# Where the softmax weights of two attention stages are scaled: VectorE before, ScalarE after

## The chip, the core and the metric

The kernel runs on one core of a Trainium2 chip. The metric is the device time of one execution in microseconds (us). Its engines are TensorE (PE in the rows; PEld is its weight load), VectorE (DVE), ScalarE (ACT), GpSimd (POOL) and the queue that issues the loads (SP). Each engine works through its own list of instructions in order; semaphores tie the lists together.

## The reference, cut to what matters

The model is two blocks deep, each with two layers, on 256 tokens of width 1024. The change touches only the attention in the mixer of the second block, which occurs twice (layers 0 and 1, the stages `mix0` and `mix1`). There are 8 heads of 64 and a single key block of 256, so the block selection picks nothing and this is left, causal attention:

```python
s_own = jnp.einsum('bhqd,bhtd->bhqt', qc, k_own) * scale
s_own = jnp.where(k_pos[None, :] <= q_pos[:, None], s_own, NEG_INF)
p = jax.nn.softmax(logits, axis=-1).astype(v.dtype)
...
merged = jax.nn.sigmoid(g_attn) * y_attn + jax.nn.sigmoid(g_conv) * y_conv
return merged @ w_out
```

Beside it the mixer computes a causal convolution of 31 taps over 512 channels, its layer norm, and the projections for q, k, v and the gates.

## The kernel before, in words

Activations lie with channels on the 128 partitions and the 256 tokens along the free dimension. The weights stream in as chunks of 128 x 2048 floats through a ring of three. For every chunk SP loads `raw`, ScalarE rounds it to a high part `wh` (`hi`, L1496), VectorE subtracts to get the low part `wl` (`lo`, L1963), and TensorE multiplies with three products, high by high, high by low and low by high (`three`, L881 to L883). A chunk of a projection is 48 matmuls on TensorE.

A mixer has 18 projection chunks (0 to 17). Chunks 10 to 17 are the gates. Around them the attention is written out by hand in pairs of heads, p = 0 to 3:

- TensorE: `gates(11 + 2p)`, `transposes(p)` (L1378), `scores(p + 1)` (L1367), `gates(12 + 2p)`, `output(p)` (L1386, L1388). `transposes(p)` waits for `pn_made`, the scaled weights of each head.
- VectorE: `masked` (L2478) adds the mask and takes the row minimum, then some taps of the convolution (`convolve`, L2440 and L2430), then `normalise`: the inverse of the two row sums of a head (L2485) and two multiplications by it (L2487), then `lo` of the coming chunks and more taps.
- ScalarE: `exps` (L1848) with the row sums, `gates` (L1630, the sigmoid of the finished chunk, then `hi` of the chunk three ahead), `evacuate` (L1855, the transposed weights from PSUM), `upper` (L1859, the head pair's output).

A head's weights are two pieces, 128 x 128 for the first 128 queries and 128 x 256 for the last. They lie in `mpr[:, h % 2]`, the sums in `rs` and the inverses in `ri`.

The convolution is shared. VectorE has all taps of two of the four channel tiles and the last four taps of the other two; GpSimd has the first 27 taps of these (`pool_mix`, L830 the product, L832 the sum). VectorE's first tap on GpSimd's tiles waits for GpSimd's last sum:

```python
if j == POOL_TAPS:
    dve.wait_ge(pool_step.sem, pool_conv[s])
```

By the order of `taps` that is the third of the five taps that stand between `masked(3)` and `normalise(3)`.

After the loop ScalarE waits until gates 17 are done on TensorE, copies three quarters of the attention output (L1871), evacuates the last pair (L1855), and TensorE can do `output(3)`. TensorE then goes on with the sums for the convolution's norm (L1402) and the next weight chunks, which it waits for in turn.

Of the kernel before, what the change touches and what calls it, by code (L numbers as in the profile page):

```python
# [8 lines left out]
ALU = mybir.AluOpType  # L9
ACT = mybir.ActivationFunctionType  # L10
# [4 lines left out]
P = 128  # L15
# [160 lines left out]
def build(nc, A, out, upto=None):  # L176
# [5 lines left out]
    def signal(name):  # L182
        return Signal(ctx.enter_context(nc.semaphore(name)))
# [37 lines left out]
    rs = sb("rs", [P, 4, 2])  # L221
    ri = sb("ri", [P, 4, 2])
# [172 lines left out]
    score_made = signal("score_made")  # L395
    ns_made = signal("ns_made")
    p_made = signal("p_made")
    pn_made = signal("pn_made")
    pt_made = signal("pt_made")
    pt_out = signal("pt_out")  # L400
# [27 lines left out]
    for kind, s in STAGES:  # L428
        x_of[s] = xstage
        if kind == "rms":  # L430
            for g, n in ((sq_made, KT), (stat_made, 1), (root_made, 1), (rstd_made, 1)):
                g.plan(s, n)
            if s != "rms0":
                six_folded.plan(s, 1)
            if s != "final":
                if s not in DEFERRED:
                    xn_made.plan(s, KT)
                xh_made.plan(s, KT)
                xl_made.plan(s, KT)
            else:  # L440
                x_ready.plan(s, KT)
                xstage = s
        if kind == "even":
            proj_out.plan(s, 12)
            xh_made.plan(s, 1 + 4)
            xl_made.plan(s, 1 + 4)
            x_ready.plan(s, 4)
            xstage = s
            heads_of[s] = 8
        if kind == "odd":  # L450
            proj_out.plan(s, 7)
            raw_made.plan(s, KT)
            xh_made.plan(s, 8)
            xl_made.plan(s, 8)
            x_ready.plan(s, 4)
            xstage = s
            heads_of[s] = 16
        if kind == "mod":
            for g in (xn_made, xh_made, xl_made):
                g.plan(s, KT)  # L460
        if kind == "mix":
            heads_of[s] = 8
            proj_out.plan(s, 18)
            glu_made.plan(s, 1)
            conv_made.plan(s, CONV_K * 2 + (CONV_K - POOL_TAPS) * 2)
            for g, n in ((rope_pe, 4), (rope_dve, 4), (ao_made, 4), (cln_pe, 2), (cln_act, 2 + CT), (cln_dve, 1 + CT),
                         (xh_made, 2 + 2 + 4), (xl_made, 2 + 2 + 4), (merged, 4), (y_out, 4), (x_ready, 4)):
                g.plan(s, n)
            xstage = s
        if kind == "ln":  # L470
            for g, n in ((four_folded, 1), (six_folded, 1), (early_sum, 1), (early_mean, 1), (late_sum, 1), (late_moved, 1), (stat_made, 1), (dsq_made, 1), (var_made, 1), (root_made, 1),
                         (inv_made, 1), (spread, 1), (cen_made, 4), (sq_made, 4), (rstd_made, int(s != STAGES[-1][1])), (ln_made, KT),
                         (x_ready, KT)):
                g.plan(s, n)
            xstage = s
        if kind == "sq":
            y_out.plan(s, KT)
        if s in heads_of:
            for g in (score_made, ns_made, p_made, pn_made, pt_made, pt_out, pv_made):
                g.plan(s, heads_of[s])  # L480
        if kind in ("ffn", "sq"):
            steps = FF_STEPS if kind == "ffn" else FF2_STEPS
            right_out.plan(s, steps * (2 if kind == "ffn" else 1))
            if kind == "ffn":
                for g in (b_made, act_made, gate_scaled, silu_scaled):
                    g.plan(s, steps)
            for g in (a_made, h_made, hh_made, hl_made):
                g.plan(s, steps)
            tile_done.plan(s, 4)
            left_added.plan(s, KT)  # L490
            x_ready.plan(s, KT)
            xstage = s
# [994 lines left out]
    def _(act):  # L1487
# [343 lines left out]
        def act_mix(s):  # L1831
            l, c0 = int(s[3:]), base[s]
            if s == "mix0":
                act.wait_ge(ada_summed.sem, ada_summed.at("ffn3"))
            for step in MIX:
                if isinstance(step, int):
                    act_chunk(s, step, c0 + step, ACT.Sigmoid if step in (2, 3) else ACT.Copy, pm)
                    if step == 1:
                        act_ln_bias(x_of[s])

            def gates(n):
                act_chunk(s, n, c0 + n, ACT.Sigmoid, pm)

            def exps(p):
                for h in (2 * p, 2 * p + 1):
                    act.wait_ge(ns_made.sem, ns_made.at(s, h + 1))
                    for b, at in enumerate((slice(0, P), slice(P, 384))):
                        last = act.activation(mpr[:, h % 2, at], mns[:, h % 2, at], ACT.Exp, bias=nm[:, h % 2, b:b + 1], scale=-1.0,  # L1848
                                              accum_out=rs[:, h % 2, b:b + 1])
                    last.then_inc(p_made.sem, 1)  # L1850

            def evacuate(p):
                for h in (2 * p, 2 * p + 1):
                    act.wait_ge(pt_made.sem, pt_made.at(s, h + 1))
                    act.activation(mpt[:, h % 2, :], bank[6 + h % 2][:, 0:384], ACT.Copy).then_inc(pt_out.sem, 1)  # L1855

            def upper(p):
                act.wait_ge(pv_made.sem, pv_made.at(s, 2 * p + 2))
                act.activation(ao[:, p, :], bank[0][:, 0:T], ACT.Copy).then_inc(ao_made.sem, 1)  # L1859

            gates(10)
            exps(0)
            for p in range(3):
                gates(11 + 2 * p)
                evacuate(p)
                exps(p + 1)
                gates(12 + 2 * p)
                upper(p)
            act.wait_ge(chunk_used.sem, c0 + 18)
            act.wait_ge(ao_made.sem, ao_made.at(s, 3))  # L1870
            act.activation(xh[:, 0:3, :], ao[:, 0:3, :], ACT.Copy).then_inc(xh_made.sem, 1)  # L1871
            evacuate(3)
            upper(3)
            act.wait_ge(ao_made.sem, ao_made.at(s))
            act.activation(xh[:, 3, :], ao[:, 3, :], ACT.Copy).then_inc(xh_made.sem, 1)
            gates(17)
            fetch(ACT.Sqrt)
            act.wait_ge(cln_dve.sem, cln_dve.at(s, 1))
            act.activation(flat(ctmp), flat(cacc), ACT.Square).then_inc(cln_act.sem, 1)
            act.wait_ge(cln_pe.sem, cln_pe.at(s, 2))  # L1880
            act.activation(root[:, :], bank[7][:, 0:T], ACT.Sqrt, scale=1.0 / CW, bias=epsc[:, 1:2]).then_inc(cln_act.sem, 1)
            fetch(ACT.Silu)
            hi(c0 + 18 + RING)
            for ct in range(CT):
                act.wait_ge(cln_dve.sem, cln_dve.at(s, 2 + ct))
                act.activation(ctmp[:, ct, :], cacc[:, ct, :], ACT.Silu, bias=vec(1, V_CLNB + 4 * l + ct)).then_inc(cln_act.sem, 1)
            for q in range(2):
                act.wait_ge(cln_act.sem, cln_act.at(s, 4 + 2 * q))
                act.activation(xh[:, 4 + 2 * q:6 + 2 * q, :], ctmp[:, 2 * q:2 * q + 2, :], ACT.Copy).then_inc(xh_made.sem, 1)
            hi(c0 + 19 + RING)  # L1890
            for i in range(4):
                if i == 2:
                    hi(c0 + 20 + RING)
                act.wait_ge(merged.sem, merged.at(s, i + 1))
                act.activation(xh[:, 2 * i:2 * i + 2, :], xn[:, 2 * i:2 * i + 2, :], ACT.Copy).then_inc(xh_made.sem, 1)
            hi(c0 + 21 + RING)
            act.wait_ge(ada_made.sem, 2 * l + 2)
            act_scaled(s, c0 + 22, l, 2)
# [57 lines left out]
    def _(dve):  # L1956
# [172 lines left out]
        def link(ins):  # L2129

            n_step[0] += 1
            ins.then_inc(dve_step.sem, 1)
            dve.wait_ge(dve_step.sem, n_step[0])
# [280 lines left out]
        def dve_mix(s):  # L2414
# [67 lines left out]
            def normalise(p):  # L2482
                for h in (2 * p, 2 * p + 1):
                    dve.wait_ge(p_made.sem, p_made.at(s, h + 1))
                    link(dve.reciprocal(ri[:, h % 2, :], rs[:, h % 2, :]))  # L2485
                    for b, at in enumerate((slice(0, P), slice(P, 384))):
                        last = dve.tensor_scalar(mpr[:, h % 2, at], mpr[:, h % 2, at], ri[:, h % 2, b:b + 1], None, ALU.mult)  # L2487
                    last.then_inc(pn_made.sem, 1)

            masked(0)  # L2490
            convolve(TAPS_PER_STEP)
# [131 lines left out]
```

## Time and profile before

| | |
|---|---|
| time, median of 3 runs | 1790.83 us (1784.06 to 1793.79) |
| the profiled execution's own time | 1791.12 us |
| its span, first to last instruction | 1789.4 us |
| PE busy | 1742.7 us (97%) |
| DVE busy | 1367.8 us (76%) |
| ACT busy | 936.8 us (52%) |
| POOL busy | 292.7 us (16%) |
| granted TensorE clock, mean | 0.990 of full speed |
| attention pairs of `mix0` / `mix1` | about 1096 to 1154 us / 1474 to 1531 us of the span |

Busy time counts an instruction from start to end; matmuls overlap, so a busy PE is not one at its peak. What counts for the total is what TensorE waits for. The two mixers run the same code, and the times of one repeat in the other, 377.5 us later.

### The profile page before, as it was taken

The numbers are of one execution on the slowest core, as the hardware profiler recorded it, in microseconds if no ns is written. First come the engines' busy times: TensorE is split into PE (matmuls) and PEld (weight loads), VectorE is DVE, ScalarE is ACT, GpSimd is POOL, SyncE is SP. The second block draws the span as 40 slices with busy tenths as digits, with TensorE's granted clock in tenths as the row PEclk, the third lists the DMA queues.
The fourth block names the chain that finished last, engine by engine and source line by source line (L and its number), as shares of the span: only waits on it lengthen the run. The fifth ranks groups of instructions, "written<-read, shape, count | busy, mean of one in ns | idle before, by whom it ended". The sixth has DMA issues, their size and how long they took to land.

```text
span 1789.4 us, 27976 instructions
## 1 busy us (share of the span) xinstructions
PE 1742.7 (97%) x11260; PEld 1565.0 (87%) x11260; DVE 1367.8 (76%) x1830; ACT 936.8 (52%) x1173; POOL 292.7 (16%) x219
## 2 busy tenths in 40 slices
PE   6999999999999999999999999999999999999998
PEld 5888799988888888779888898898888998998887
DVE  5997654798789978686987779878755699778654
ACT  6554464655455544566554444756543536555433
POOL 1000100220210001050000139610000089010000
PEclk9999999999999999999999999999999999999999
DMA  7777433376667766524676643353555344335551
GB/s 270 277 254 268 175 143 118 138 267 259 246 249 290 261 223 247 212 95 174 236 266 247 231 165 141 125 182 129 188 193 193 122 153 157 139 127 200 188 190 48
DMA packets 53232, 348.28 MB, mean 195 GB/s; under 512 B 6769, under 2 KB 10114, under 8 KB 13058
## 3 DMA queue, kind: packets, MB, share of 16 engines
q1 hardware_dynamic: 53122, 346.73, 53.0%
q8 instruction: 80, 1.31, 0.3%
q14 instruction: 30, 0.25, 0.0%
HBM read 345.65 MB, written 1.05 MB: 194 GB/s over the span
## 4 chain that ended last, share of the span: by engine, by line
PE 89%; DVE 7%; ACT 2%; issue 1%; POOL 1%; DMA 0%; SPq 0%; ACTq 0%; DVEq 0%; POOLq 0%
PE bank L926 39%; PE bank L925 21%; PE bank L881 7%; PE bank L882 7%; PE bank L883 7%; DVE wl L1963 2%; ACT wh L1496 1%; DVE bank L2440 1%; PE bank L896 1%; DVE arena L2459 1%; PE bank L1429 1%; PE bank L906 0%; DVE arena L2458 0%; DVE arena L2487 0%; DMA raw<-in_chunks 0%
## 5 line engine op out<-in xcount | busy, mean ns | idle before, releaser
L1963 DVE TENSOR_TENSOR wl<-raw,wh 128x2048 fp32r<-128x2048 f32 (+1 forms) x279 | 640.1, 2296 | 252.7 <-ACT wh L1496 252.0
L926 PE MATMUL bank<-xx,wh 128*128 128x512 f32 x1920 | 674.5, 395 | 0.0
L1496 ACT ACTIVATE wh<-raw 128x2048 fp32r<-128x2048 f32 (+1 forms) x279 | 526.2, 1886 | 204.4 <-PE bank L926 174.0
L925 PE MATMUL bank<-xx,wl 128*128 128x256 f32 x1920 | 541.2, 282 | 14.9 <-DVE wl L1963 14.9
L926 PEld LDWEIGHTS bank<-xx,wh 128*128 128x128 f32 x1920 | 361.1, 188 | 83.4
L926 PE MATMUL bank<-hx,wh 128*128 128x512 f32 x1216 | 422.0, 390 | 0.0
L925 PEld LDWEIGHTS bank<-xx,wl 128*128 128x128 f32 x1920 | 364.1, 190 | 16.2 <-issue 14.9
L925 PE MATMUL bank<-hx,wl 128*128 128x256 f32 x1216 | 343.4, 282 | 1.2 <-DVE wl L1963 1.2
L881 PE MATMUL bank<-xx,wh 128*128 128x256 f32 x1008 | 293.1, 291 | 2.5 <-ACT arena L1630 1.4
L882 PE MATMUL bank<-xx,wh 128*128 128x256 f32 x1008 | 286.6, 284 | 0.0
L883 PE MATMUL bank<-xx,wl 128*128 128x256 f32 x1008 | 286.4, 284 | 0.0
L926 PEld LDWEIGHTS bank<-hx,wh 128*128 128x128 f32 x1216 | 228.3, 188 | 47.9
L925 PEld LDWEIGHTS bank<-hx,wl 128*128 128x128 f32 x1216 | 229.8, 189 | 1.5 <-DVE wl L1963 1.5
L881 PEld LDWEIGHTS bank<-xx,wh 128*128 128x128 f32 x1008 | 194.4, 193 | 11.6 <-issue 8.0
L882 PEld LDWEIGHTS bank<-xx,wh 128*128 128x128 f32 x1008 | 194.5, 193 | 0.5 <-issue 0.2
L883 PEld LDWEIGHTS bank<-xx,wl 128*128 128x128 f32 x1008 | 194.4, 193 | 0.0
L847 POOL TENSOR_TENSOR arena<-xn 128x512 f32<-128x512 f32 x8 | 15.5, 1937 | 746.2 <-ACT xn L1505 685.2
L2040 DVE CUSTOM_DVE_ANT_0 arena<-arena,csil 128x1024 f32<-128x1024 f32 x96 | 114.8, 1233 | 0.0
L832 POOL TENSOR_TENSOR arena<-arena 128x512 f32<-128x512 f32 x52 | 110.1, 2117 | 4.1
L1630 ACT ACTIVATE arena<-bank 128x512 f32<-128x512 f32 x48 | 28.6, 597 | 108.8 <-PE bank L883 108.6
L1580 ACT ACTIVATE arena<-bank 128x512 f32<-128x512 f32 x44 | 26.4, 599 | 100.1 <-PE bank L926 100.1
L855 POOL TENSOR_TENSOR arena<-x 128x512 f32<-128x512 f32 x4 | 9.2, 2296 | 384.5 <-DVE x L2115 289.9
(332 smaller groups left out, 1955.6 us busy)
## 6 DMA issues: line engine op xcount, KB each, us to landing
raw<-in_chunks SPq DMA_DIRECT2D x263, 1024.0 KB, 4.8
arena<-in_ada SPq DMA_DIRECT2D x48, 1024.0 KB, 4.9
raw<-in_chunks SPq DMA_DIRECT2D x16, 768.0 KB, 4.2
arena<-in_bias_rows SPq DMA_DIRECT2D x1, 2048.0 KB, 17.9
x<-in_x SPq DMA_DIRECT2D x4, 256.0 KB, 4.1
arena<-in_w_uk SPq DMA_DIRECT2D x1, 1024.0 KB, 4.9
arena<-in_w_uv SPq DMA_DIRECT2D x1, 1024.0 KB, 10.6
out<-x SPq DMA_DIRECT2D x8, 128.0 KB, 2.1
```

Of the source, the lines that this page charges most:

```text
L832: pool.tensor_tensor(acc, acc, ptmp[:, b, :, :], ALU.add).then_inc(pool_step.sem, 1)
L881: pe.matmul(o, wa, ma, start=start, stop=False, **kw)
L882: pe.matmul(o, wa, mb, start=False, stop=False, **kw)
L883: return pe.matmul(o, wb, ma, start=False, stop=stop, **kw)
L896: pe.matmul(bank[5][:, 0:P], ident[:, :], ident[:, :], start=True, stop=True)
L925: pe.matmul(o[:, 0:T], lo_w, halves[:, 0, :], start=start, stop=False, skip_group_check=True)
L926: return pe.matmul(o.rearrange("p (h t) -> p h t", h=2), hi_w, halves, start=False, stop=stop, skip_group_check=True)
L1496: act.activation(wh[:, c % RING, at], raw[:, c % RING, at], ACT.Copy).then_inc(hi_made.sem, 1)
L1580: act.activation(ra, psum[:, 4:6, T:2 * T], ACT.Copy).then_inc(right_out.sem, 1)
L1630: act.activation(pj[:, n, :], bank[2 + n % 2][:, :], func).then_inc(proj_out.sem, 1)
L1963: dve.tensor_tensor(wl[:, c % RING, at], raw[:, c % RING, at], wh[:, c % RING, at].bitcast(F32), ALU.subtract).then_inc(lo_made.sem, 1)
L2040: last = dve.tensor_tensor_reduce(w, w, csil[:, :], 1.0, 0.0, ALU.mult, ALU.add, dots[:, n % 2, j:j + 1])
```

## The change

In both mixers VectorE's `normalise` keeps only the inverse of the sums, signalled by a new semaphore `ri_made`. The two multiplications of each head become two ScalarE copies with a per-partition scale, in a new ScalarE `normalise(p)` that stands directly behind `exps(p)`, ahead of the sigmoid and `hi` that followed. ScalarE signals `pn_made` now. The attention of the first block (`act_pairs`, `dve_pairs`) is as it was.

```diff
         if kind == "mix":
+            ri_made.plan(s, 8)
...
+            def normalise(p):
+                for h in (2 * p, 2 * p + 1):
+                    act.wait_ge(ri_made.sem, ri_made.at(s, h + 1))
+                    for b, at in enumerate((slice(0, P), slice(P, 384))):
+                        last = act.activation(mpr[:, h % 2, at], mpr[:, h % 2, at], ACT.Copy, scale=ri[:, h % 2, b:b + 1])
+                    last.then_inc(pn_made.sem, 1)
...
             gates(10)
             exps(0)
+            normalise(0)
             for p in range(3):
                 gates(11 + 2 * p)
                 evacuate(p)
                 exps(p + 1)
+                normalise(p + 1)
                 gates(12 + 2 * p)
                 upper(p)
...
             def normalise(p):
                 for h in (2 * p, 2 * p + 1):
                     dve.wait_ge(p_made.sem, p_made.at(s, h + 1))
-                    link(dve.reciprocal(ri[:, h % 2, :], rs[:, h % 2, :]))
-                    for b, at in enumerate((slice(0, P), slice(P, 384))):
-                        last = dve.tensor_scalar(mpr[:, h % 2, at], mpr[:, h % 2, at], ri[:, h % 2, b:b + 1], None, ALU.mult)
-                    last.then_inc(pn_made.sem, 1)
+                    dve.reciprocal(ri[:, h % 2, :], rs[:, h % 2, :]).then_inc(ri_made.sem, 1)
```

## Rows read from the trace of the kernel before

**Rows 1.** The page: the chain that ended last, shares of the span by engine

```profile
PE 89%; DVE 7%; ACT 2%; issue 1%; POOL 1%; DMA 0%; SPq 0%; ACTq 0%; DVEq 0%; POOLq 0%
```

**Rows 2.** Waits of TensorE, whole span: us in total, times, longest

```profile
PE bank L1378 <- DVE arena L2487: 5.4, 4, 1.8
...
PE bank L1386 <- ACT arena L1855: 1.7, 2, 0.9
```

**Rows 3.** Timeline of TensorE, mix0, first pair: start, us, what, [idle before <-releaser]

```profile
1103.75 0.55 PE L1378 MATMUL bank<-ident,arena 128*128 128x128 f32 x3 [0.65 <-DVE arena L2487]
1106.11 0.90 PE L1378 MATMUL bank<-ident,arena 128*128 128x128 f32 x3 [1.81 <-DVE arena L2487]
1106.94 1.66 PE L1367 MATMUL bank<-arena 64*128 64x128 f32 x8
```

**Rows 4.** Windows: length, busy of PE, PEld, DVE, ACT, POOL, PEclk, DMA share, GB/s

```profile
1096.00:1150.00 54.00, 51.55 (x413) 47.11 (x411) 49.66 (x103) 37.73 (x63) 50.66 (x32) 0.97 0.43 157
...
1106.00:1109.40 3.40, 3.29 (x15) 2.31 (x16) 3.40 (x6) 1.79 (x3) 3.40 (x2) 0.50 0.12 14
```

**Rows 5.** Timeline of VectorE, mix0, first pair

```profile
1102.01 0.15 DVE L2485 RECIPROCAL ri<-rs 128x2 f32<-128x2 f32 x1
1102.20 1.50 DVE L2487 TENSOR_SCALAR arena<-arena,ri 128x128 f32<-128x128 f32 x2
...
1103.81 2.25 DVE L2487 TENSOR_SCALAR arena<-arena,ri 128x128 f32<-128x128 f32 x2
1105.97 2.28 DVE L1963 TENSOR_TENSOR wl<-raw,wh 128x2048 fp32r<-128x2048 f32 x1
```

**Rows 6.** Groups by form, ScalarE, 1096 to 1175: xcount, busy, mean ns, idle before

```profile
L1848 ACT ACTIVATE arena<-arena,nm 128x256 f32<-128x256 f32 x8 | 4.0, 495 | 0.0
...
L1848 ACT ACTIVATE arena<-arena,nm 128x128 f32<-128x128 f32 x8 | 3.2, 394 | 11.5 <-DVE nm L2478 11.5
```

**Rows 7.** Timeline of VectorE, mix0, last pair

```profile
1147.95 1.28 DVE L2430 SCALAR_TENSOR_TENSOR arena<-arena,vecT 128x256 f32<-128x256 f32 x3 [4.05 <-POOL arena L832]
1149.14 0.16 DVE L2485 RECIPROCAL ri<-rs 128x2 f32<-128x2 f32 x1
```

**Rows 8.** Timeline of ScalarE, mix0, last pair

```profile
1144.47 1.28 ACT L1630 ACT_TABLE_LOAD   x1
...
1148.06 0.38 ACT L1859 ACTIVATE arena<-bank 128x256 f32<-128x256 f32 x1
1150.31 0.84 ACT L1871 ACTIVATE xx<-arena 128x768 fp32r<-128x768 f32 x1 [1.88 <-PE bank L883]
1151.06 0.85 ACT L1855 ACTIVATE arena<-bank 128x384 f32<-128x384 f32 x2
```

**Rows 9.** Timeline of TensorE, mix0, last pair

```profile
1150.11 1.04 PE L1378 MATMUL bank<-ident,arena 128*128 128x128 f32 x6
1151.97 0.65 PE L1386 MATMUL bank<-arena 128*64 128x256 f32 x4 [0.82 <-ACT arena L1855]
```

**Rows 10.** Timeline of GpSimd, mix0, beside the first pair's scaling

```profile
1102.51 1.04 POOL L830 TENSOR_TENSOR arena<-arena,vecT 128x512 f32 x1
1103.63 1.28 POOL L832 TENSOR_TENSOR arena<-arena 128x512 f32<-128x512 f32 x1
1104.85 1.05 POOL L830 TENSOR_TENSOR arena<-arena,vecT 128x512 f32 x1
1105.98 3.40 POOL L832 TENSOR_TENSOR arena<-arena 128x512 f32<-128x512 f32 x1
```

**Rows 11.** Timeline of GpSimd, mix0, its last product and sum

```profile
1145.49 1.04 POOL L830 TENSOR_TENSOR arena<-arena,vecT 128x512 f32 x1
1146.61 1.30 POOL L832 TENSOR_TENSOR arena<-arena 128x512 f32<-128x512 f32 x1
```

**Rows 12.** Timelines of mix1's last pair, VectorE and TensorE

```profile
1525.41 1.28 DVE L2430 SCALAR_TENSOR_TENSOR arena<-arena,vecT 128x256 f32<-128x256 f32 x3 [4.04 <-POOL arena L832]
...
1529.49 0.65 PE L1386 MATMUL bank<-arena 128*64 128x256 f32 x4 [0.89 <-ACT arena L1855]
```

More of the change, by code:

```diff
@@ L397, in build @@
     p_made = signal("p_made")
+    ri_made = signal("ri_made")
     pn_made = signal("pn_made")
```

## The prediction, made before the result was known

> **What bounds the kernel now.** I read the page's chain first. It lies 89% on TensorE [rows 1], so an edit on VectorE or ScalarE counts only where TensorE waits for them. The list of TensorE's waits says where that is: the transposes of the mixers waited 5.4 us in all for VectorE's scaling L2487, in four places, and the output products waited 1.7 us for ScalarE's evacuation L1855, in two [rows 2]. The timelines then place them. All of the first wait is at the first pair: in mix0 TensorE stood 0.65 us and then 1.81 us [rows 3]. Behind these idle times its granted clock was 0.50 for 3.4 us, which is the 1.2 GHz level [rows 4], and eight score matmuls took 1.66 us there [rows 3]. The second wait is at the last pair, 0.82 us in mix0 and 0.89 us in mix1 [rows 9, 12]. Between the two TensorE is never held up by the scaling. So two questions matter per mixer: what the edit gives at the first pair, and what it does at the last, where VectorE itself stands 4.05 us, until GpSimd's last tap is summed, before it comes to the inverses [rows 7].
>
> **What leaves VectorE.** A head loses two multiplications. Where GpSimd runs beside them they take 1.50 and 2.25 us for the two heads [rows 5], 3.75 us a pair; the eight inverses stay. That is about 3.7 us for each of the first three pairs. The next subtraction L1963 can start at about 1102.4 instead of 1105.97 [rows 5]. No transfer is moved: SP's loads follow these subtractions, and an earlier one only frees a slot of the ring sooner. In the middle pairs the freed time is worth nothing by itself, since TensorE doesn't wait there.
>
> **What comes to ScalarE.** The trace has no scaled copy of this size. The nearest rows are the exponentials over the same tiles with a per-partition operand, 394 and 495 ns [rows 6]. An instruction on ScalarE starts before its forerunner ends: L1871 took 0.84 us and its follower started 0.75 us after it [rows 8], an overlap of 0.09. So a head costs 0.394 + 0.495 - 2 x 0.09 = 0.71 us, a pair 1.42 us. As bounds I take 1.2 us (no price for the pointer operand: the 128x256 evacuation takes 0.38 [rows 8]) and 1.8 us (no overlap). I take 1.42. I add no load of a function table for the copies themselves, because the copies L1855 run in the timeline between other functions without one.
>
> **The first pair, a gain of about 3.9 us that has to survive.** The first head's inverse is there at 1102.16 [rows 5], the exponentials are done by then, and the copies of the two heads end at about 1102.95 and 1103.65. TensorE ends its gates at 1103.75 - 0.65 = 1103.1, so it transposes at once and again at 1103.7, and does the scores by 1105.0. The next gates start at about 1105.05 instead of at the end of the slow scores, 1106.94 + 1.6 = 1108.53 [rows 3], and at the 2.4 GHz level: 3.5 us, and 0.4 us more from the first gate matmuls, which ran slow. If nothing took it back this would be 2 x 3.9 = 7.8 us.
>
> **The middle pairs, nothing.** ScalarE's sigmoid and `hi` now stand behind the copies, and VectorE's `lo` waits for `hi`, so the two engines are tied more closely. But ScalarE was busy 37.7 of 54 us in this stretch [rows 4] and gains 4 x 1.42 = 5.7 us, while the chunk that a late `hi` belongs to is needed two gate blocks later. I put the last pair's masks and exponentials where they were, within 2 us. What hides that lateness is the next wait.
>
> **The last pair, a loss of 4.4 us.** GpSimd's last sum ends at 1147.9 [rows 11]. It isn't touched by the edit, as its rows next to the scaling show below. VectorE's order is unchanged too, so it still stands before the third tap until 1147.95, and the inverses of the last pair come at 1149.14 to 1149.30 and up to about 1149.5 [rows 7]. Before, ScalarE did not care: it was through with the exponentials and loaded the sigmoid's table at 1144.47 (1.28 us), did the sigmoid of gates 16, `hi` and `upper(2)`, the last starting at 1148.06 [rows 8], all of it inside VectorE's wait. Now its copies, which wait for these inverses, stand ahead of all that. This is the new wait, and what is queued behind it is: the table load, sigmoid, `hi`, L1859, L1871 and the evacuation L1855 that TensorE's `output(3)` needs. Step by step: copies start 1149.35 and end their issue at 1150.77; table load to the end of L1859's issue, from 1144.47 to 1148.43 before, 3.96 us, now up to 1154.73; L1871 0.75 us to 1155.48; two evacuations 0.85 us to 1156.33; TensorE starts at 1156.4. It started at 1151.97 [rows 9]: +4.4 us. TensorE can't use the time, its list is in order. It arrives early instead: 3.9 us ahead it ends gates 17 near 1146.2 and would then stand for the inverses, so the first pair's gain is waited away. From `output(3)` on TensorE's chain is as tight as before, all that waits there waits for TensorE, and the delay stays. Two mixers: +8.8 us. mix1 has the same waits, 4.04 and 0.89 us [rows 12].
>
> **The clock.** TensorE would now stand near 4 us before the last transposes and near 5 us behind them, with under 1 us of work between. At the first pair 2.46 us of idle with 0.55 us of work in it were followed by 3.4 us at half clock [rows 3, 4], which cost half of it, 1.7 us. The old dip is in the gain that is lost; a new one falls where TensorE resumes, at `output(3)`, and costs 1.7 us per mixer. Bounds: nothing, and 3.4 us (two such stretches). I take 1.7, 3.4 us for both. The Trainium skill, "TensorE: Matmul & The Clock Gate", section "HAM oscillation", warns that idle gaps of TensorE throttle the clock for the work that follows; this trace agrees with its dip.
>
> **The sum.** 1791.1 (the profiled execution's own time, 0.3 above the median of the runs shown) + 8.8 + 3.4 = 1803.3 us, +0.7%.
>
> **Rivals.** (a) GpSimd comes free earlier. VectorE's multiplications and GpSimd's taps meet in the rows: a pair of multiplications took 1.50 and 2.25 us beside GpSimd. If GpSimd also lost time to them, the taps would end sooner without them, by at most the pure work of three pairs. Against it: GpSimd's starts beside the scaling are 1.12, 1.22 and 1.13 us apart, and in the undisturbed end 1.12 [rows 10, 11]. What lengthens its sums to 3.40 is the subtraction L1963 [rows 5, 10], and as many of these run as before. Pure work of a pair is some 1.1 us (the last pair, with GpSimd done, took 0.55 a head), so 3.3 us sooner, a loss of 1.1 + 1.7 us per mixer: 1796.7 us. The Trainium skill, "SBUF — State Buffer", section "Who interferes with whom", states it as a rule: VectorE's tensor_scalar in a two-port mode takes an exclusive lock, and GpSimd blocks for the whole instruction. By it the time would be that of (a); this trace shows only the other direction, VectorE waiting.
>
> (b) Faster: the first pair's gain reaches the end. It would need TensorE alone to set the last pair, that is inverses, sigmoid, `hi` and both copies over before TensorE ends gates 17. That decides only if GpSimd's last sum came more than 8 us sooner, before about 1140. Price -3.9 per mixer: 1783.3 us, which is not over 0.5% either. For it speaks only that the first pair's wait is real.
>
> (c) No clock loss: the work between the idle times keeps the clock up, or the slow stretch ends before TensorE resumes. 1799.9 us, at the edge of what can be told.
>
> (d) The scaled copy needs a table of its own, 1.28 us more in each last pair, or dips of two stretches: 1805.9 and 1806.7 us.
>
> **How the numbers follow.** A change of under 0.5% (9 us) can't be told from none in this kernel; three runs before lay 9.7 us apart. Chances: my forecast 0.60, (a) 0.10, (b) 0.03, (c) 0.15, (d) 0.12. The forecast is 1803.3 us; with its own bounds it lies in 1799 to 1807. The range takes in (a) and (d): 1796.5 to 1808. Slower by over 0.5%: the forecast and (d), less a part for scatter, and half of (c): 0.73. Within 0.5%: (a), half of (c) and the scatter: 0.24. Faster: 0.03.
>
> **What would show it.** Right: in both mixers TensorE's transposes of the first pair without idle time and no half clock behind them; GpSimd's last sum at about 1147.9 still and VectorE's wait for it of some 4 us or more; ScalarE idle some 3 to 5 us in front of the last pair's copies, released by VectorE's L2485; the sigmoid of gates 16 at about 1152 instead of 1145.76; TensorE idle for about 4 us before L1378 and about 5 us before L1386, then half clock. Wrong: if GpSimd ends well before 1147; if `output(3)` starts near 1152; or if a middle pair shows TensorE waiting for scaled weights or for `wl`, which would make the loss larger.

## The result, and the profile after

The changed kernel took 1799.51 us (median of 9 runs, 1797.12 to 1803.71), the kernel before 1787.44 us in the runs beside it (1784.06 to 1793.79). The ratio is 1.0058, interval 1.0048 to 1.0069: slower by 0.6%. The forecast was 1803.3 us, slower, range 1796.5 to 1808.

TensorE's waits over the whole span of the changed kernel (line, released by, us in total, times, longest):

```profile
PE bank L1388 <- ACT arena L1864: 9.9, 2, 5.1
PE bank L1380 <- ACT arena L1858: 5.1, 5, 2.1
```

These answer to [rows 2]. The wait for the scaled weights (L1380) is as long as before, 5.1 against 5.4 us, but now ends by ScalarE's copies L1858. The wait for the evacuation, L1388, which was 1.7 us, is 9.9 us. That is where most of the time went. TensorE's timeline in mix0 shows the order:

```profile
1093.49 0.93 PE L1369 MATMUL bank<-arena 64*128 64x128 f32 x8
...
1100.32 1.24 PE L1380 MATMUL bank<-ident,arena 128*128 128x128 f32 x6
...
1108.29 0.65 PE L1388 MATMUL bank<-arena 128*64 128x256 f32 x4
...
1129.52 1.24 PE L1380 MATMUL bank<-ident,arena 128*128 128x128 f32 x6 [0.23 <-ACT arena L1858]
...
1132.12 0.39 PE L883 MATMUL bank<-xx,wh 128*128 128x256 f32 x1 [0.51 <-ACT arena L1632]
...
1146.99 1.59 PE L1380 MATMUL bank<-ident,arena 128*128 128x128 f32 x6 [2.12 <-ACT arena L1858]
1153.36 1.12 PE L1388 MATMUL bank<-arena 128*64 128x256 f32 x4 [4.77 <-ACT arena L1864]
...
1158.00 0.47 PE L883 MATMUL bank<-xx,wh 128*128 128x256 f32 x1
...
1161.06 1.89 PE L1415 MATMUL bank<-arena,ones 128*128 128x256 f32 x8
```

The first transposes (1100.32) have no idle time in front, unlike [rows 3]. The last stand behind 2.12 us, and `output(3)` behind 4.77 us. To compare kernels I measure from the first scores of the mixer, here 1093.49. `output(3)` starts at +59.9 us, and chunk 18, the next weight chunk, at +64.5 us (1158.00). The kernel before has these lines:

```profile
1096.24 0.93 PE L1367 MATMUL bank<-arena 64*128 64x128 f32 x8
...
1154.41 0.47 PE L881 MATMUL bank<-xx,wh 128*128 128x256 f32 x1
...
1158.55 1.99 PE L1413 MATMUL bank<-arena,ones 128*128 128x256 f32 x8 [0.92 <-ACT arena L1879]
...
1201.24 1.03 PE L915 MATMUL bank<-x,ones 128*128 128x256 f32 x4
```

So there chunk 18 starts at +58.2 us and `output(3)` [rows 9] at +55.7. mix0 is 6.3 us longer up to chunk 18, mix1 too (64.98 against 58.66): 12.7 us in all. Not all of it lasts. Halfway through chunk 18 the kernel before waits 0.92 us for ScalarE's square of the convolution's norm (L1413, released by L1879), in both mixers; the changed kernel, coming later, does not wait there (L1415). At L915, TensorE's sums of x that come near the mixer's end (L917 in the changed kernel, at 1203.67 and 1588.55), the changed kernel is 5.2 and 5.8 us behind, 11.0 us in all. The whole profiled span grew by 8.6 us, 1798.0 against 1789.4: the code outside was some 2 us shorter in this execution, and such scatter is in every pair of executions (the nine runs of before lie 9.7 us apart).

VectorE in the last pair of the changed kernel, which answers to [rows 7], and GpSimd's last sum, to [rows 11]:

```profile
1144.76 1.28 DVE L2441 SCALAR_TENSOR_TENSOR arena<-arena,vecT 128x256 f32<-128x256 f32 x3 [1.66 <-POOL arena L834]
1145.95 0.22 DVE L2496 RECIPROCAL ri<-rs 128x2 f32<-128x2 f32 x2
```

```profile
1143.43 1.29 POOL L834 TENSOR_TENSOR arena<-arena 128x512 f32<-128x512 f32 x1
```

ScalarE at the same place, which answers to [rows 8]:

```profile
1146.14 1.49 ACT L1858 ACTIVATE arena<-arena,ri 128x128 f32<-128x128 f32 x4 [2.50 <-DVE ri L2496]
1147.65 1.28 ACT L1632 ACT_TABLE_LOAD   x1
1148.94 0.60 ACT L1632 ACTIVATE arena<-bank 128x512 f32<-128x512 f32 x1
1149.44 1.90 ACT L1498 ACTIVATE wh<-raw 128x2048 fp32r<-128x2048 f32 x1
1151.24 0.38 ACT L1868 ACTIVATE arena<-bank 128x256 f32<-128x256 f32 x1
1151.70 0.84 ACT L1882 ACTIVATE xx<-arena 128x768 fp32r<-128x768 f32 x1
1152.45 0.85 ACT L1864 ACTIVATE arena<-bank 128x384 f32<-128x384 f32 x2
```

Read from the top: ScalarE stands 2.50 us until VectorE's inverses, which stand behind VectorE's wait for GpSimd. Then copies, table load, sigmoid, `hi`, L1868, L1882, and only then the evacuation that TensorE waits for. From the inverses (1145.95) to `output(3)` (1153.36) it is 7.4 us. The clock in two windows (columns as in [rows 4]):

```profile
1147.70:1157.90 10.20, 5.43 (x18) 3.78 (x19) 1.82 (x4) 8.39 (x11) 0.00 (x0) 0.50 0.01 2
1157.90:1161.00 3.10, 3.10 (x26) 3.00 (x25) 2.61 (x2) 2.75 (x4) 0.00 (x0) 0.99 0.00 0
```

TensorE's clock was granted at 0.50 for 10.2 us, through the wait and 4.5 us beyond the start of `output(3)`.

### The profile page after: what moved, and what is told of

It is laid out like the page before. It is cut to its first block, busy times and chain, and to the rows that moved or that the text cites. A ratio compares the mean times of both kernels' runs of the same rounds, so it can differ in the third digit from the quotient of the medians.

```text
span 1798.0 us, 27976 instructions
## 1 busy us (share of the span) xinstructions
PE 1743.2 (97%) x11260; PEld 1563.3 (87%) x11260; DVE 1347.7 (75%) x1798; ACT 948.4 (53%) x1205; POOL 291.2 (16%) x219
## 4 chain that ended last, share of the span: by engine, by line
PE 77%; issue 11%; POOL 6%; DVE 3%; ACT 2%; POOLq 0%; DMA 0%; SPq 0%; ACTq 0%; DVEq 0%
PE bank L928 38%; PE bank L927 20%; PE bank L883 5%; PE bank L884 4%; PE bank L885 4%; POOL arena L832 4%; ACT wh L1498 1%; DVE wl L1974 1%; PE bank L898 1%; PE bank L1431 0%; PE bank L908 0%; POOL arena L834 0%; DMA raw<-in_chunks 0%; PE bank L1404 0%; PE bank L1224 0%
## 5 line engine op out<-in xcount | busy, mean ns | idle before, releaser
L927 PE MATMUL bank<-xx,wl 128*128 128x256 f32 x1920 | 540.7, 282 | 15.1 <-DVE wl L1974 14.8
L834 POOL TENSOR_TENSOR arena<-arena 128x512 f32<-128x512 f32 x52 | 105.1, 2022 | 4.1
```

What stands on the lines that cost most here:

```text
L834: pool.tensor_tensor(acc, acc, ptmp[:, b, :, :], ALU.add).then_inc(pool_step.sem, 1)
L927: pe.matmul(o[:, 0:T], lo_w, halves[:, 0, :], start=start, stop=False, skip_group_check=True)
```

## The experiments

Nine kernels, each timed beside the kernel before: the first four (from "last pair on VectorE" to "spare matmuls, 12 + 30") on one chip, the next three on a second, the last two on a third. Positions are those of mix0 and mix1 in the one profiled execution of each kernel, in us behind the mixer's first scores, worked out from the timelines. The last column is L915 or L917, near the mixer's end.

| kernel | ratio to before, interval | `output(3)` | chunk 18 | near the end |
|---|---|---|---|---|
| before | 1 | 55.7, 56.2 | 58.2, 58.7 | 105.0, 105.5 |
| changed | 1.0058, 1.0048 to 1.0069 | 59.9, 60.3 | 64.5, 65.0 | 110.2, 111.3 |
| last pair on VectorE | 1.0012, 1.0001 to 1.0023 | 56.9, 56.3 | 61.0, 60.2 | 106.6, 106.3 |
| last inverses early | 1.0024, 1.0009 to 1.0038 | 58.3, 57.7 | 62.8, 62.4 | 108.4, 108.2 |
| last copies later | 1.0031, 1.0021 to 1.0041 | 58.1, 57.5 | 62.8, 62.2 | 109.0, 108.1 |
| spare matmuls, 12 + 30 | 1.0054, 1.0041 to 1.0068 | 62.2, 61.8 | 64.6, 64.2 | 111.5, 111.1 |
| spare matmuls, 9 + 20 | 1.0037, 1.0023 to 1.0052 | 59.7, 60.3 | 62.1, 62.8 | 109.0, 109.6 |
| first pair only on ScalarE | 0.9999, 0.9988 to 1.0011 | 55.6, 56.2 | 60.3, 60.9 | 106.1, 106.9 |
| last pair reordered | 1.0009, 0.9998 to 1.0019 | 53.7, 53.1 | 56.2, 56.6 | 109.5, 108.5 |
| the same, norm first | 0.9982, 0.9970 to 0.9994 | 52.7, 53.1 | 56.1, 56.6 | 103.2, 103.6 |
| this order, scaling on VectorE | 1.0002, 0.9993 to 1.0012 | 55.4, 55.8 | 57.8, 58.2 | 105.5, 105.9 |

### The last pair back on VectorE

```diff
                 exps(p + 1)
-                normalise(p + 1)
+                if p < 2:
+                    normalise(p + 1)
```

On VectorE heads 6 and 7 get the inverse and both multiplications as before.

> Pairs 0 to 2 as in the changed kernel, the last pair's scaling back on VectorE. My theory (the whole loss comes from the last pair's copies, which wait on ScalarE in front of everything that output(3) needs): output(3) starts 55.5 to 56.5 us behind the mixer's first scores, as in the kernel before (55.7), instead of 59.9; TensorE waits some 3 to 4 us in front of the last transposes, and one stretch of half clock may stand there. Total equal to before, up to 3 us above it: ratio 0.999 to 1.002. Rival (ScalarE's extra copies cost in every pair, by late hi and wl): three quarters of the loss stay, ratio 1.004 or more.

Measured: 1.0012, chunk 18 at 61.0 and 60.2. Four fifths of the loss are gone with one pair of four. What is left, 1.0012 (1.0001 to 1.0023), is what ScalarE's copies in the other three cost on balance. The trace shows how: the last pair's masks start 3.0 and 1.9 us later than before (at +48.65 and +48.06 us against +45.68 and +46.12), and ScalarE's exponentials and all that is queued behind them follow. `output(3)` is 0.1 to 1.2 us later than before; TensorE waited for ScalarE there:

```profile
PE bank L1388 <- ACT arena L1864: 4.1, 2, 2.7
...
PE bank L1380 <- DVE arena L2502: 2.7, 2, 1.9
```

### The two halves of the new wait

The copies are late for two reasons in a row: VectorE brings the inverses late, and ScalarE has its other work behind them. One run removes the first half:

```diff
-                convolve(TAPS_PER_STEP)
-                normalise(p + 1)
+                if p == 2:
+                    convolve(2)
+                    normalise(3)
+                    convolve(TAPS_PER_STEP - 2)
+                else:
+                    convolve(TAPS_PER_STEP)
+                    normalise(p + 1)
```

> VectorE inverts the last pair's sums behind two taps, ahead of the three taps that wait for GpSimd. My theory: the inverses come some 2.4 us sooner, the copies end 2.4 us sooner, and output(3) starts 57.4 us behind the first scores instead of 59.9; the wait in front of the last transposes nearly goes, the one in front of output(3) stays near 4.8 us, because table load, sigmoid and hi still stand behind the copies. Total 5 to 7 us under the changed kernel, so ratio to before 1.002 to 1.003. Rival (the late inverses, that is GpSimd, are the whole cause): output(3) back at 56 or less, ratio 1.000 or less.

The other removes the second:

```diff
-                normalise(p + 1)
+                if p < 2:
+                    normalise(p + 1)
                 gates(12 + 2 * p)
                 upper(p)
+            normalise(3)
```

> ScalarE's copies of the last pair stand behind the sigmoid and hi of gates 16 and behind upper(2), VectorE as in the changed kernel. My theory: the copies start 1.5 us later than in the changed kernel, but nothing of the 4 us queue is behind them, so output(3) starts 57.2 us behind the first scores instead of 59.9. Total 5 to 7 us under the changed kernel, ratio to before 1.002 to 1.003. Rival (the moved scaling itself is what costs, wherever it stands): no change from the changed kernel, ratio 1.005 or more.

Measured: 1.0024 and 1.0031, with `output(3)` 1.6 to 2.6 us and 1.8 to 2.8 us earlier than in the changed kernel. Either half gives back about half of the loss, a little less than expected in both (57.4 and 57.2 us for `output(3)`, 1.002 to 1.003). In the first the last copies start 1.6 and 2.6 us sooner, where 2.4 was expected, and `output(3)` with them. Neither alone brings `output(3)` back to 56 us, so neither the late inverses nor what is queued behind the copies is the whole cause; it is the two in series.

### The clock

```diff
                 gates(11 + 2 * p)
+                if p == 3:
+                    pe.wait_ge(ns_made.sem, ns_made.at(s, 8))
+                    keep_clock(12)
                 transposes(p)
                 if p < 3:
                     scores(p + 1)
                     gates(12 + 2 * p)
+                else:
+                    keep_clock(30)
```

> The changed kernel, with 12 spare 128x128 matmuls on TensorE in front of the last transposes and 30 in front of output(3), which fill its idle time there and change nothing else. Theory: the idle time costs the clock as well; in the changed kernel some 4.5 us of half clock fall behind the start of output(3), 2.2 us of loss per mixer. With the matmuls the clock stays at full, output(3) starts as late as before (59.9 us behind the first scores), and the total falls by 3 to 5 us: ratio to before 1.003 to 1.004. Rival (the clock costs nothing here, or falls elsewhere instead): no change, ratio 1.006; or more, if the spare matmuls delay the chain.

Measured: 1.0054, a miss. The clock held, but the matmuls took longer than the idle time and put `output(3)` 1.5 to 2.3 us later, as much as the clock gave. With 9 and 20 instead:

> As the run with spare matmuls, but 9 and 20 of them, since 12 and 30 took longer than the idle time and put output(3) 2.3 us later. Theory (the clock takes some 2.2 us per mixer): output(3) at 59.9 us as in the changed kernel, full clock, chunk 18 at 62.3 instead of 64.5; total 4 to 5 us under the changed kernel, ratio to before 1.003 to 1.004. Rival: chunk 18 stays at 64.5, ratio 1.006.

Measured: 1.0037. `output(3)` stands where it stood in the changed kernel, chunk 18 is 2.4 and 2.2 us earlier, and the window over the wait reads

```profile
1147.00:1156.00 9.00, 8.69 (x72) 8.01 (x71) 2.58 (x6) 7.85 (x14) 0.00 (x0) 1.00 0.00 0
```

granted clock 1.00 instead of 0.50. So the slow clock behind the wait is worth 2.3 us per mixer up to chunk 18. Part of it is lost again, since TensorE, coming earlier, now waits 0.92 us for the square of the norm: near the mixer's end the gain is 1.2 and 1.7 us. The ratios, 1.0037 and 1.0058, agree with a gain but don't prove it: their intervals overlap and they come from different chips.

### Only the first pair on ScalarE

The copies of pairs 1 to 3 go back to VectorE (`ri_made` only for heads 0 and 1; `normalise(0)` stays on ScalarE, `normalise(p + 1)` is dropped there).

> Only the first pair scaled on ScalarE, the three others on VectorE as before. Theory (the first pair gives some 3.9 us to TensorE, which it then waits away in front of the last transposes because GpSimd's taps end when they did; the middle pairs tie ScalarE's hi to VectorE's wl without price): the first pair's wait and its half clock are gone, TensorE idles 3 to 4 us before the last transposes, output(3) at 55.7 us, ratio 0.998 to 1.001, and the same as with only the last pair on VectorE within 2 us. Rival (the gain reaches the end): output(3) at 52 us, ratio 0.996 or less.

Measured: 0.9999, `output(3)` at 55.6 and 56.2, as before. TensorE's waits from 1090 to 1165 us:

```profile
PE bank L1380 <- DVE arena L2500: 2.5, 2, 2.1
PE bank L1380 <- ACT arena L1858: 0.6, 1, 0.6
```

The first pair's gain is there and is waited away at the last pair, in 2.1 us of idle time before the last transposes (3 to 4 were expected). In the profiled execution chunk 18 is even 2.1 and 2.3 us later than before, with a granted clock of 0.52 over 6.7 us there (1148.1 to 1154.8 in mix0). TensorE then does not wait for the square of the norm, and near the mixer's end it is 1.1 and 1.4 us later. The totals don't show even that (ratio 0.9999, and this execution's own span was 1789.0 us against 1789.4). That is no more than the scatter of the code outside, so whether this kernel loses anything stays open.

### Does the scaling pay on ScalarE when the order fits?

All pairs on ScalarE, the last inverses early as above, and ScalarE's end written by who waits:

```diff
                 normalise(p + 1)
-                gates(12 + 2 * p)
+                if p < 2:
+                    gates(12 + 2 * p)
                 upper(p)
+            evacuate(3)
             act.wait_ge(chunk_used.sem, c0 + 18)
...
-            evacuate(3)
             upper(3)
...
+            gates(16)
             gates(17)
```

TensorE waits for all sigmoids only ahead of the third of the next four chunks, which reuses their banks, and for `upper(3)` ahead of the first.

> Scaling on ScalarE in all pairs, with both causes of the new wait taken away: the last inverses ahead of the taps that wait for GpSimd, and on ScalarE the last evacuation straight behind the last copies and upper(2), with the sigmoid and hi of gates 16 behind the attention's end; TensorE waits for the sigmoids only where it reuses their banks. My theory (only the order around the last pair made the change slow; the first pair's gain is real): the last transposes start about 51.5 us behind the first scores instead of 53.9, output(3) about 53 instead of 55.7, and chunk 18 at 56 to 57 instead of 58.2, where the last taps of the convolution are next to bind. Total 2 to 5 us under the kernel before, ratio 0.997 to 0.999. Rival (copies on ScalarE cost something that isn't in that order): ratio 1.001 or more.

Measured: 1.0009, a miss: 0.997 to 0.999 was expected, and the rival's ratio was 1.001 or more. Chunk 18 came at 56.2 and 56.6, as expected, 2 us ahead of the kernel before; the total did not follow. TensorE's waits, whole span:

```profile
PE bank L1417 <- ACT arena L1894: 8.2, 2, 4.6
```

L1894 is the square for the convolution's norm. It had been moved behind two sigmoids and two `hi`, the same mistake as the change's, one step further on. Half clock followed here too (0.50 from 1157.6 to 1160.0), and near the mixer's end it was 4.5 and 3.0 us later than before. So the last order:

```diff
-            gates(16)
-            gates(17)
+            hi(c0 + 16 + RING)
             fetch(ACT.Sqrt)
             act.wait_ge(cln_dve.sem, cln_dve.at(s, 1))
             act.activation(flat(ctmp), flat(cacc), ACT.Square).then_inc(cln_act.sem, 1)
+            hi(c0 + 17 + RING)
             act.wait_ge(cln_pe.sem, cln_pe.at(s, 2))
             act.activation(root[:, :], bank[7][:, 0:T], ACT.Sqrt, ...).then_inc(cln_act.sem, 1)
+            act_out_of(s, 16, c0 + 16, ACT.Sigmoid, pm)
+            act_out_of(s, 17, c0 + 17, ACT.Sigmoid, pm)
             fetch(ACT.Silu)
```

> The reordered kernel again (scaling on ScalarE), with ScalarE's work behind the attention sorted by who needs it first: hi of chunk 19, the square for the convolution's norm, hi of chunk 20, the root, and only then the sigmoids of gates 16 and 17. In the first reordering the square stood behind both sigmoids and TensorE waited 4.6 us for it. Theory: chunk 18 starts 56.2 to 56.6 us behind the first scores as there (58.2 in the kernel before), TensorE's wait for the square falls from 4.6 and 3.6 to under 1 us, and no half clock follows. Total 4 to 8 us under the kernel before, ratio 0.996 to 0.998. Rival (the moved scaling costs elsewhere): ratio 1.000 or more.

Measured: 1784.50 us against 1788.56, ratio 0.9982, interval 0.9970 to 0.9994: faster than both kernels, by 3 to 4 us against the kernel before, where 4 to 8 were expected. TensorE in mix0:

```profile
1093.81 0.93 PE L1369 MATMUL bank<-arena 64*128 64x128 f32 x8
...
1144.95 0.93 PE L1380 MATMUL bank<-ident,arena 128*128 128x128 f32 x6
1146.46 0.65 PE L1388 MATMUL bank<-arena 128*64 128x256 f32 x4 [0.58 <-ACT arena L1866]
...
1148.31 1.99 PE L1404 MATMUL bank<-arena,ones 128*128 128x256 f32 x8 [0.98 <-DVE arena L2447]
1153.01 1.89 PE L1417 MATMUL bank<-arena,ones 128*128 128x256 f32 x8
...
1164.80 0.36 PE L883 MATMUL bank<-xx,wh 128*128 128x256 f32 x1 [1.27 <-DVE xx L2562]
```

The last transposes start without idle time at +51.1 us (before +53.9), the square's wait is gone, and what is late next is L1404's input, the convolution's last taps on VectorE (0.98 us). Behind it is a wait that the kernel before does not have: 1.27 us in each mixer for VectorE's low part of the convolution's output (L2562). In this order the two sigmoids and one more table load (1155.43 to 1157.82 in mix0) stand on ScalarE ahead of the activations that feed it.

The control has the same order with all scaling on VectorE:

> The same order of ScalarE, TensorE and the last inverses, but all scaling on VectorE as in the kernel before. It tells what the place of the scaling is worth once the order around it is right. Theory (the first pair's 3.9 us on TensorE then count, until the convolution's last taps bind): this one keeps the first pair's wait and its half clock, and starts chunk 18 at 57.0 to 57.8 us, about 1 us later than with the scaling on ScalarE; ratio 0.998 to 0.9995, and 1 to 3 us above the run with the scaling on ScalarE. Rival (the place is worth nothing, only the order): both within 1 us.

Measured: 1.0002, 1789.57 us. That is 5.1 us above the run with the scaling on ScalarE by the medians, 3.6 by the two ratios; 1 to 3 were expected, and a ratio under 1. The intervals of the two ratios to before hardly touch (0.9993 to 1.0012 and 0.9970 to 0.9994), and both kernels ran on the same chip. Chunk 18 is 1.7 us later in each mixer, and near the mixer's end it is 2.3 and 2.4 us: 4.7 us of the 5.1. The new order alone is worth nothing that can be told, and the traces say why: it is 0.4 us ahead of the kernel before at chunk 18, but waits 1.3 us for the same low part (L2554) and is 0.4 to 0.5 us behind near the end. The moved scaling is worth something once the order fits. The first pair's waits stand in the control as in the kernel before:

```profile
1102.33 0.55 PE L1378 MATMUL bank<-ident,arena 128*128 128x128 f32 x3 [0.67 <-DVE arena L2493]
1104.68 0.55 PE L1378 MATMUL bank<-ident,arena 128*128 128x128 f32 x3 [1.80 <-DVE arena L2493]
```

## Why the prediction was right, point by point

**The copies' price.** 1.42 us a pair forecast. The changed kernel's forms read (xcount, busy, mean ns, idle before)

```profile
L1858 ACT ACTIVATE arena<-arena,ri 128x256 f32<-128x256 f32 x8 | 4.0, 494 | 0.0
L1858 ACT ACTIVATE arena<-arena,ri 128x128 f32<-128x128 f32 x8 | 3.2, 395 | 4.2 <-DVE ri L2496 4.2
```

the same as the exponentials' 495 and 394 ns [rows 6], four in 1.50 us from first start to last end (1.51 us until the next instruction starts), and no table load in front of them. Rival (d)'s first half is out.

**The first pair, +3.9 us forecast.** `output(0)` starts 14.8 us behind the first scores (1108.29 - 1093.49) and 18.6 before (1114.86 - 1096.24): 3.8 us. Right; the runs with only the first and with all but the last pair on ScalarE show that without a new order at the end it is worthless.

**The middle pairs, nothing forecast.** Not quite; the forecast's own sign against it, a middle pair that waits for scaled weights, is there. VectorE's freed time turned into waits for ScalarE's `hi`, twice 5.2 us:

```profile
1118.18 3.01 DVE L1974 TENSOR_TENSOR wl<-raw,wh 128x2048 fp32r<-128x2048 f32 x1 [5.22 <-ACT wh L1498]
```

and in the third pair TensorE waited 0.23 us for scaled weights and 0.51 us for a sigmoid. It reached the last transposes 2.5 us early (1144.87, +51.4 against +53.9), not 3.9, and idled 2.1 us there instead of near 4. The last pair's masks came 1.9 us later than before, just within the 2 us allowed, so VectorE waited 1.66 us for GpSimd and ScalarE 2.50 us for the inverses, where 4 and 3 to 5 were named as signs. As forecast, the next wait hides all that in the changed kernel; the run with only the last pair on VectorE pays for some of it.

**The last pair, +4.4 us forecast.** 4.1 us in both mixers, through the very steps that were summed: 7.4 us from the inverses to `output(3)`, 7.3 forecast. The two halves were then each shown by a run of their own.

**The clock, +1.7 us per mixer forecast.** 2.2 us measured: from `output(3)` to chunk 18 it took 4.64 us (1158.00 - 1153.36) against 2.44. The size was set by one stretch of 3.4 us at half clock; the changed kernel has 10.2 us, of which 4.5 lie behind the start of `output(3)`. The term was 0.5 us too small per mixer. The spare matmuls, which keep the clock, give the same 2.3 us. Rival (c) is out, the second half of (d) partly in.

**Behind `output(3)`, nothing forecast.** This step was wrong. The prediction had TensorE's chain there "as tight as before", so that the whole delay stays. The kernel before has a slack of 0.92 us in each mixer, the wait for the norm's square at L1413, and the changed kernel uses it up: of the 6.3 us at chunk 18, 5.2 and 5.8 us are left near the mixer's end.

**GpSimd.** Its last sum ends at +51.2 us, before +51.7. Rival (a) wanted it 3.3 us sooner and is out. The Trainium skill, "SBUF — State Buffer", section "Who interferes with whom", says that of VectorE and GpSimd the one that issues first holds the shared ports and the other blocks. That allows either direction, so the prediction read it too narrowly when it gave GpSimd all of the time. The traces show GpSimd gaining 0.4 us in the changed kernel and 0.7 us between the last two runs. What stretches its sums most is still the subtraction `lo`: the longest take 3.2 us with the scaling gone, up to 3.4 us before, 1.3 us alone.

**The sum.** 12.2 us forecast; 12.7 us at chunk 18 of the two mixers in the profiled execution, 11.0 us near their ends, 12.1 us between the medians, 10.4 us by the ratio. That it is so close is in part luck: the clock was put 0.5 us too low per mixer, and the slack behind `output(3)`, 0.5 to 1.2 us, was left out. The forecast time of 1803.3 us is 3.8 us high because it started from 1791.1 us, where the kernel before took 1787.44 us beside the changed one.

**Rival (b)**, the gain that reaches the end, is false for the change as made and half true with another order: there TensorE does set the last pair, but 2.0 to 2.1 us of the 3.9 arrive at chunk 18 and 1.8 to 1.9 near the mixer's end. The forecast put its condition on GpSimd alone, 8 us sooner; it can be met with GpSimd as it is, by taking the inverses out from behind GpSimd's taps and sorting ScalarE's list.

## What to carry to other kernels

When work moves from one engine to another, cost what stands behind it in the new engine's list, not its own length: 1.5 us of copies moved `output(3)` by 4.1 us, because they waited for something late and everything that TensorE needed stood behind them. Look for such waits at the end of a pipelined loop, where the next iteration no longer covers. A gain at the head of a stretch reaches its end only if nothing on the way is set by another engine; find the last such place first and order each engine's list there by who waits for it. Last, follow a delay up to the old kernel's next wait and not only to where it arises: 0.92 us of it vanished in one here.

## What the runs showed of the hardware

The idle time of TensorE cost more than its length: with 2.12 and 4.77 us of it and 1.6 us of work between, the granted clock stayed at 0.50 (1.2 GHz) for 10.2 us, and spare matmuls in the idle time gave back 2.3 us per mixer up to chunk 18, as long as they fitted (9 and 20; with 12 and 30 `output(3)` came 1.5 to 2.3 us later). A scaled copy with a per-partition factor takes ScalarE as long as an exponential of the same form, 395 and 494 ns. The same multiplications took VectorE up to 2.25 us a head beside GpSimd [rows 5] and 0.55 us a head in the last pair with GpSimd done; with them gone GpSimd's last sum came only 0.4 to 0.7 us sooner in a mixer.
